# A two-block model on one core: ScalarE takes some of the weight rounding, decay products spread over the attention heads, and a spare PSUM bank for grouped products

## The reference

```
for l in 0..1:                                  # first block
    h = rms_norm(x)*(1+scale)+shift             # scale, shift from c @ ada_w
    p = h @ w_in                                # shifted features, pool features, two gates
    y_a = gated delta-rule recurrence (8 heads of 64) over p
    y_b = (trailing means over 2,4,8,16 tokens - token) @ pool_w
    x += gate1 * ((g_a*(y_a@proj_a) + g_b*(y_b@proj_b)) @ w_out)
    x += gate2 * (silu(h2@w_g) * (h2@w_u)) @ w_down
for l in 0..1:                                  # second block
    u = rms_norm(h); gq,gk,gv,gg,ra,aq,ak,av,gate_a,gate_b = split(u @ w_in2)
    la = log_sigmoid(ra @ w_alpha_up + b)/16    # decays, two directions, 4 heads
    a = gated linear attention, both directions, chunks (4 heads), normed, * silu(gg)
    b = softmax attention (8 query heads, 2 key heads), rotary positions
    h += norm((sig(gate_a)*(a@w_o_gla) + sig(gate_b)*(b@w_o_attn)) @ w_out2)
    h += norm(feed-forward(h));  h += norm(sigmoid(h@w_ple_gate) * (p@w_ple_proj))
```

## Time and profile before

| | us |
|---|---|
| median of 3 runs | 3852.53 (3851.03 to 3856.24) |
| the profiled execution, its own time | 3852.76 |
| its span, first to last instruction | 3850.8 |
| TensorE busy | 3707.2 (96%) |
| VectorE busy | 1803.9 (47%) |
| GpSimd busy | 2275.8 (59%) |
| ScalarE busy | 851.9 (22%) |

### The profile page before, as it was taken

One profiled execution on the slowest core, in us unless ns is written; L12 is line 12 of the kernel. 1 busy time (PEld: TensorE's weight loads), 2 busy tenths in 40 slices (PEclk: granted clock), 3 DMA queues, 4 the chain that ended last, 5 costly groups with the idle time before them and its releaser, 6 DMA issues.

```text
span 3850.8 us, 52946 instructions
## 1 busy us (share of the span) xinstructions
PE 3707.2 (96%) x21300; PEld 3007.9 (78%) x21300; DVE 1803.9 (47%) x2338; ACT 851.9 (22%) x1334; POOL 2275.8 (59%) x2222
## 2 busy tenths in 40 slices
PE   5999999999999999999999999999999999999997
PEld 4887778887787678888887678888778876778886
DVE  5654653234744753124453654523464446453335
ACT  3322110004222110003321532000253225220002
POOL 4613777786513777774656356777645553667773
PEclk9999999999999999998999999999989999999999
DMA  5223444342223443332223132333312331323332
GB/s 187 88 84 108 148 142 145 118 147 77 75 84 108 139 147 109 96 99 64 79 80 118 52 104 83 98 96 98 100 52 83 104 94 55 110 82 98 96 97 70
DMA packets 192483, 386.60 MB, mean 100 GB/s; under 512 B 21488, under 2 KB 21616, under 8 KB 190576
## 3 DMA queue, kind: packets, MB, share of 16 engines
q1 hardware_dynamic: 170064, 338.77, 29.2%
q10 hardware_dynamic: 22176, 44.45, 3.3%
HBM read 362.16 MB, written 20.97 MB: 99 GB/s over the span
## 4 chain that ended last, share of the span: by engine, by line
PE 86%; DVE 9%; ACT 3%; DMA 1%; issue 1%; ACTq 0%; SPq 0%; DVEq 0%
PE psum L420 18%; PE psum L422 18%; PE psum L421 18%; PE psum L485 3%; PE psum L487 3%; PE psum L486 3%; PE psum L507 2%; PE psum L444 2%; PE psum L445 2%; PE psum L452 1%; PE psum L975 1%; PE psum L950 1%; PE psum L604 1%; PE psum L592 1%; PE psum L808 1%; PE psum L809 1%
## 5 line engine op out<-in xcount | busy, mean ns | idle before, releaser
L2241 POOL TENSOR_SCALAR w_hi<-raw 128x512 fp32r<-128x512 f32 x1084 | 745.6, 688 | 1434.4 <-DMA raw<-weight_chunks 1430.8
L2243 POOL TENSOR_TENSOR w_lo<-raw,w_hi 128x512 fp32r<-128x512 f32 x1084 | 1494.3, 1379 | 90.4
L420 PE MATMUL psum<-in_hi,w_hi 128*128 128x512 f32 x1920 | 760.4, 396 | 9.4 <-ACT hs L1319 3.1
L421 PE MATMUL psum<-in_lo,w_hi 128*128 128x512 f32 x1920 | 748.2, 390 | 0.0
L422 PE MATMUL psum<-in_hi,w_lo 128*128 128x512 f32 x1920 | 747.8, 389 | 0.0
L420 PEld LDWEIGHTS psum<-in_hi,w_hi 128*128 128x128 f32 x1920 | 360.8, 188 | 97.6 <-issue 11.1
L421 PEld LDWEIGHTS psum<-in_lo,w_hi 128*128 128x128 f32 x1920 | 360.9, 188 | 79.8 <-issue 6.2
L422 PEld LDWEIGHTS psum<-in_hi,w_lo 128*128 128x128 f32 x1920 | 360.8, 188 | 75.4
L485 PE MATMUL psum<-in_hi,w_hi 128*128 128x512 f32 x576 | 253.9, 441 | 1.5 <-ACT sg L1354 1.5
L486 PE MATMUL psum<-in_lo,w_hi 128*128 128x512 f32 x576 | 225.7, 392 | 0.0
L487 PE MATMUL psum<-in_hi,w_lo 128*128 128x512 f32 x576 | 225.6, 392 | 0.0
(11 more groups left out here) (421 smaller groups left out, 6759.8 us busy)
## 6 DMA issues: line engine op xcount, KB each, us to landing
raw<-weight_chunks SPq DMA_DIRECT2D x1084, 256.0 KB, 2.6
ada_col<-ada_slabs SPq DMA_DIRECT2D x80, 512.0 KB, 4.1
spill<-gate_st ACTq DMA_DIRECT2D x56, 256.0 KB, 2.7
ada_at<-ada_slabs SPq DMA_DIRECT2D x8, 1024.0 KB, 15.6
gin<-spill ACTq DMA_DIRECT2D x32, 256.0 KB, 3.1
mgs<-spill ACTq DMA_DIRECT2D x32, 256.0 KB, 2.7
sml<-small ACTq DMA_DIRECT2D x4, 1024.0 KB, 5.3
spill<-nt ACTq DMA_DIRECT2D x16, 256.0 KB, 2.6
```

What stands on the lines that cost most here:

```text
L420: pe.matmul(bank[:], wh, hi[:, i, :], start=(i == 0), stop=False)
L421: pe.matmul(bank[:], wh, lo[:, i, :], start=False, stop=False)
L2241: ts(w_hi[:, slot, :], raw[:, slot, :], 1.0, 1.0, ALU.mult, ALU.mult).then_inc(sem("chunk_hi"), 1)
L2243: ins = tt(w_lo[:, slot, :], raw[:, slot, :], w_hi[:, slot, :].bitcast(F32), ALU.subtract)
```

## The change

Four edits.

1. **Rounding.** In two stretches of each layer pair (recurrence to pool products in the first block, the four heads' cores in the second) ScalarE instead of GpSimd rounds `w_hi`, a 128 x 512 copy, for 136 of the 1084 chunks. It does so in program order, ahead of its wait for a job, for all chunks up to three past the one at which TensorE will be when that job ends (`CAST_LEAD = 4`). GpSimd waits for `cast_ready` and only subtracts.
2. **Decays split.** Decays 2 and 3 move from before core(0) to behind core(0) and core(1), on TensorE, ScalarE and VectorE. `gla_factors(0)` waits only for decay 1.
3. **Spare bank.** `group`'s third product goes to bank 3.
4. **Fill.** `FILL_CORE` goes from (5, 2, 2, 15) to (4, 4, 4, 14), and a ninth side job (the first of the eight `g2b`) runs in the linear attention, instead of later in the softmax attention.

```diff
+CAST_LEAD = 4
-FILL_CORE = (5, 2, 2, 15)
+FILL_CORE = (4, 4, 4, 14)
...
+        def scalar_casts():
+            return [s for first, end in zip(casts_from, casts_to) for s in range(first + CAST_LEAD + 1, end)]
...
             def group(members, key):
-                stepped(members, key, ("lin",) * len(members), "lin")
+                stepped(members, key, ("lin", "lin", "bg"), "lin")
...
-                side_jobs([(("g2a", l, m), "w_in2", l, N_GA + m) for m in range(DT)], "bg2")
+                side_jobs([(("g2a", l, m), "w_in2", l, N_GA + m) for m in range(DT)]
+                          + [(("g2b", l, 0), "w_in2", l, N_GB)], "bg2")
                 gla_in(l, 0, h_in, 0, 1)
-                gla_decay(l, 2)
-                gla_in(l, 1, h_in, 3)
+                gla_in(l, 1, h_in)
                 lane[0] = "lin2"
+                casts_from.append(len(chunks))
                 for h in range(GH):
                     gla_core(l, h)
                     if h + 2 < GH:
+                        gla_decay(l, h + 2)
                         gla_in(l, h + 2, h_in)
-                fill(DT * DT)
+                fill(DT * (DT + 1))
+                casts_to.append(len(chunks))
...
+            def casts_before(job):
+                while cast_done[0] < len(casts) and casts[cast_done[0]] < closed_at[job] + CAST_LEAD:
+                    s = casts[cast_done[0]]
+                    slot = slice(s % RING * CHUNK, (s % RING + 1) * CHUNK)
+                    act.wait_ge(sem(f"chunk_in{s % RING}"), 16 * (s // RING + 1))
+                    af(w_hi[:, slot, :], raw[:, slot, :], ACT.Copy).then_inc(sem("cast_ready"), 1)
+                    act.wait_ge(sem("cast_ready"), passed("cast_ready", s))
+                    cast_done[0] += 1
...
-                    else:
-                        act.wait_ge(sem("cum_ready"), count("cum_ready", (l, GH - 1, 1)))
+                    act.wait_ge(sem("cum_ready"), count("cum_ready", (l, max(h, 1), 1)))
...
-                pool.wait_ge(sem(f"chunk_in{s % RING}"), 16 * (s // RING + 1))
-                ts(w_hi[:, slot, :], raw[:, slot, :], 1.0, 1.0, ALU.mult, ALU.mult).then_inc(sem("chunk_hi"), 1)
-                pool.wait_ge(sem("chunk_hi"), s + 1)
+                if s in casts:
+                    pool.wait_ge(sem("cast_ready"), count("cast_ready", s))
+                else:
+                    pool.wait_ge(sem(f"chunk_in{s % RING}"), 16 * (s // RING + 1))
+                    ins = ts(w_hi[:, slot, :], raw[:, slot, :], 1.0, 1.0, ALU.mult, ALU.mult)
+                    ins.then_inc(sem("chunk_hi"), 1)
+                    pool.wait_ge(sem("chunk_hi"), passed("chunk_hi"))
```

More of the change, by code:

```diff
@@ L288, in emit @@
         windows_at = []
+        casts_from = []
+        casts_to = []
+        closed_at = {}
+        def scalar_casts():
+            return [s for first, end in zip(casts_from, casts_to) for s in range(first + CAST_LEAD + 1, end)]
         def ada_in_ffn(l, mm):
@@ L382, in close @@
                 closed[name] = len(closed)
+                closed_at[name] = len(chunks)
                 for s in touched:
@@ L932, in block2 @@
                                hi=go_hi, lo=go_lo)
-                side_jobs([(("g2b", l, m), "w_in2", l, N_GB + m) for m in range(DT)], "bg2")
+                side_jobs([(("g2b", l, m), "w_in2", l, N_GB + m) for m in range(1, DT)], "bg2")
                 lane[0] = "lin2"
@@ L1104, in _ @@
             stored = [0]
+            casts = scalar_casts()
+            cast_done = [0]
+            def casts_before(job):
[6 more added lines that the diff above has]
+                    cast_done[0] += 1
             def gates_before(job, stage):
@@ L1109, in gates_before @@
                     gate = side_order[stored[0]]
+                    casts_before(gate)
                     act.wait_ge(*done(gate))
@@ L1119, in gates_before @@
                     stored[0] += 1
+                casts_before(job)
             def gate_back(dst, gate):
@@ L1443, in block2 @@
                 gla_in(l, 0, 0, 1)
-                gla_decay(l, 2)
-                gla_in(l, 1, 3)
+                gla_in(l, 1)
                 gla_factors(l, 0)
@@ L1449, in block2 @@
                     if h + 2 < GH:
+                        gla_decay(l, h + 2)
                         gla_in(l, h + 2)
                 gates_before(("p2a", l, 0), gate_st2)
-                act.wait_ge(sem("gate_out"), count("gate_out", ("g2a", l, DT - 1)))
+                act.wait_ge(sem("gate_out"), count("gate_out", ("g2b", l, 0)))
                 act.dma_start(rope_t[:], rope).then_inc(sem("rope_in"), 16)
@@ L2109, in block2 @@
                     dve.wait_ge(sem("vector_step"), passed("vector_step"))
-                for h in range(GH):
-                    gla_decay(l, h)
+                gla_decay(l, 0)
+                gla_decay(l, 1)
                 gla_keys(l, 0)
@@ L2114, in block2 @@
                     gla_core(l, h)
+                    if h + 2 < GH:
+                        gla_decay(l, h + 2)
                 for m in range(DT):
@@ L2230, in pool_window @@
                 pool.wait_ge(sem("pooled_ready"), passed("pooled_ready", (l, d)))
+            casts = set(scalar_casts())
             for s in range(len(chunks)):
```

## The result

The changed kernel takes 3885.30 us, median of 6 runs (3883.39 to 3889.98); beside them the kernel before took 3855.89 (6 runs, 3851.03 to 3863.52). The ratio is 1.0076, 95% interval 1.0062 to 1.0090: slower by 29 us. The profiled execution took 3884.6, its span is 3882.8, and the mean granted clock of TensorE is 0.975, where before it was 0.982.

What follows compares the result with a forecast made beforehand. TensorE, busy 3707.2 of 3850.8 us, was taken as the bound. 3852.8 + 25.6 + 11.4 + 2 - 8.3 - 3.6 - 7.0 - 3 + 2 = 3871.9, about 3872 us; range 3855 to 3886.

Steps and rivals of the forecast that it cites:

- the forecast's own bounds: Whole kernel: the forecast itself, about 3872 us, bounded at 3861 to 3882, chance 0.67.
- the rival of a late ScalarE: Cores' gv: every gv waits 2.5 us instead of 0.5, half clock follows; 3887 us, chance 0.13.
- The bank: Late decays behind `gn`: second product waits for bank 7 until VectorE's `ot<-psum`, 6.4 us at four places, +25.6.
- The clock behind it: Behind the four bank waits: a stretch at half clock costs 2.85 us each, +11.4 (bounds 6.8 and 14).
- The gains: Spare bank -8.3, head of core(0) -3.6, before `p2a` -7.0, roundings in the recurrence -3.
- +4 against them: Late gv chunks behind the bank, +2, and GpSimd catching up beside VectorE at the ends of the stretches, +2.
- The spare bank's 8.3: Fourth product behind `group`: waits for ScalarE's bank read (3.1, 3.1, 2.1) go, -8.3, no clock added.
- the `go_lo` wait of 5.3: Before `p2a`: longer last fill covers this wait, and its half-clock stretch (1.7) goes too, -7.0 together.
- `kd` gave 1.3 of 3.6: Head of core(0), before `gst`: `kd` ready earlier, less a shorter fill; net 1.8 in two layers, -3.6 (0 to -9.2).
- the norm's `mt` 1.6 of 3: Recurrence: ScalarE's roundings relieve VectorE, cutting about a third of the norm's 8.0 us of waits, -3.
- ScalarE late: Cores' gv: decay and roundings queued on ScalarE make a late chunk cost 0.5 us at four places, +2 (0 to 10).
- Roundings: ScalarE's roundings: -3 in the recurrence (-8 to +4), and part of the -3.6 at the head of core(0).

## Why the prediction came out as it did

The direction, the main cause and its place were right. 3885.3 lies in the range, less than 1 us from its upper end, and that is partly luck: the forecast's own bounds were 3861 to 3882, and the range went on to 3886 for the rival of a late ScalarE, which didn't come. The step from before was 32 us in the profiled execution (29 by the medians) where the sum said 19. Term by term:

- **The bank** (25.6 said; 19.8 of waits, 24.0 with the products). The mechanism is shown by the split alone. At the first place the wait ends where the prediction had it, 7.4 us behind the start of the last product of `gn` (said 7.3), but it begins later, and is 5.3 long instead of 6.3. That product keeps TensorE for 0.95 us (1883.07 to 1884.02), not 0.45 as I read from the earlier trace rows; and the first `gz` takes 1.06 us by itself. I had halved the 1.06 of the earlier trace rows, but there the two products run side by side in that time; apart, each takes it. So the pair also costs 1.06 more work at each place, 4.2 in all, for which the sum has no term.
- **The clock behind it** (11.4 said, about 13 measured). The four stretches are 36.7 us long, but part of them lies in the wait, which is counted already. TensorE is busy for 25.8 us of them, and half of that is lost: 12.9, an estimate from the rows above. Bank and clock together are 37.0 said and 36.9 measured; that it is so close is luck, since the one is too large by 1.6 and the other too small by 1.5. The split alone gives 37.0 by the same count.
- **The gains** (-8.3, -3.6, -7.0, -3, and +4 against them: -17.9 said; 32.0 - 36.9 = -4.9 measured, or -7.5 by the medians). This is where the sum failed: it took a removed wait for won time. The spare bank's 8.3 and the `go_lo` wait of 5.3 are gone; `kd` gave 1.3 of 3.6, the norm's `mt` 1.6 of 3. That is 16.5, but the waits other than those for `ot` fell by only 11.4 in all, since others grew, and outside the four places the clock costs some 9 us more (27.8 - 18.4 in the profiled execution), 6.7 of it in the preparation. Alone, the spare bank measures +-0 instead of -8.3: its waits fall by 3.6 in all, and the clock takes that back. The fill measures +4 instead of -7.0: its waits came back as others.
- **ScalarE late** (+2; the rival said +17): 1.1 us of waits for the subtraction. That rival is excluded in the change. It came true in another kernel, with the decay behind the keys.
- **Roundings** (-3 in the recurrence, part of the -3.6 in the core): by themselves -7, about as said, though by the table nearly half of it is clock (-3.6) and not waits. The waits for `mt` behind the weights of the stretch ends stay (11.7, now 11.9).

On the exclusive lock of VectorE and GpSimd, which the prediction cites from the Trainium skill (SBUF — State Buffer, section Who interferes with whom): the traces agree. Where GpSimd is idle, `qd` and `kd` take 0.69 each, and `kd` 1.71 beside a subtraction.

The mean granted clock shifts between executions of one kernel: 0.977 to 0.983 with the spare bank alone, 0.979 to 0.983 before. The Trainium skill (TensorE: Matmul & The Clock Gate, section Part 1: The HAM clock gate) says that the clock's monitor runs freely and isn't reset when a kernel starts, so that the same kernel differs from run to run. These executions agree that it differs; whether that is the reason, or what decides the stretch of the preparation, no run here shows.

## What to carry to other kernels

Before moving work behind another stage, list which buffer each moved instruction will ask for and who frees it last: the bank here was freed at the end of a chain of four steps across two engines, and moving the work further on only changed the engine that was late. On a TensorE that is busy 96% of the time, count a wait for its length and again for the work that runs at half clock behind it: here 5.0 and 3.2 us a place, and the second hardly fell when the wait was halved. And a removed wait of a microsecond is not yet won time: read the sum of all waits, and the mean granted clock of several executions, before believing in it.

## What was not expected of the hardware

Five us of useless products in place of a wait of 5 us made the kernel with the late decays 14 us faster. At three of four places a wait of some 2.6 us brought a stretch of 6.6 us at half clock, as long as a wait of some 5 us did at three of four. A stretch of 10 to 14 us at half clock appears in a preparation in which TensorE has no wait above 0.4 us in the 12 us ahead of it (in the trace of the change), in some traces and not in others of programs that are equal up to that point. Two products of 16 rows each that use different rows run side by side in 1.06 us; one after the other each takes that long.
